# Adding the S5 state outputs in their bank by products with the identity, with u5 in halves

## The chip, the cores and the metric

The kernel runs on one core of a Trainium2 chip. The metric is the device time of one execution in microseconds (us); lower is better. A core has five engines that run side by side and meet only at semaphores: TensorE (PE, matmuls, with its weight loads shown apart as PEld), VectorE (DVE), ScalarE (ACT), GpSimd (POOL) and SyncE (SP), which here only issues DMAs. PE writes to PSUM, eight banks of 128 x 512 f32; DVE and ACT read them out.

## The reference

One step of a one-layer decoder on 256 prompt tokens and 8 x 8 sample tokens (T = 320 columns), all in f32: RMS norm, a mixer of two branches, attention over a memory of 256 tokens, and a mixture of 32 experts. The change is in the second branch of the mixer, S5, a diagonal complex state space model on 64 groups of 16 channels with 64 states each:

```python
lam_bar = jnp.exp(lam * step)
b_bar = ((lam_bar - 1.0) / lam)[..., None] * lax.complex(b_re, b_im)
bu = jnp.einsum('gnk,blgk->blgn', b_bar, ug)
bu = bu.at[:, 0].add(lam_bar * h0)
_, states = lax.associative_scan(combine, (a, bu), axis=1)     # x[l] = lam_bar * x[l-1] + bu[l]
y = jnp.real(jnp.einsum('gkn,blgn->blgk', c, states)) + d * ug
```

Here ug is u5, one slice of the input projection `rms_norm(x) @ w_in`. The first branch, SSD, takes other slices: xbc (1536 channels, a causal convolution over 4 tokens and silu), dt (softplus) and z.

## The kernel before

**S5 by chunks.** The tokens are cut into chunks of Q = 8, which gives 40 chunks (NCK): 32 of the prompt and 8 of the samples. u5T holds u5 by position in the chunk: 128 partitions x (8 positions, 8 tiles of 128 channels, 40 chunks). Three steps make the output:

- `chunk_in` (jobs hi0 to hi7, L1670): the input of each state in a chunk, by products of a table with ug. ug is u5T regrouped: SP writes u5T to DRAM (L639) and reads it back in eight pieces (L642). hi0 to hi3 need channels of the tiles 0 to 3 only, hi4 to hi7 those of the tiles 4 to 7.
- DVE: a scan over the chunks for each half of the states (`scan`, L2633 to L2644, needs hi3 or hi7) and the table of output weights (`step_out`, L2652 to L2656). `hprev` then holds the state at the start of each chunk.
- Output of a tile ft of channels, two parts. The in-chunk part, job fy (L1754), is the product of tap tables `ks` with lagged copies `ux` of u5. The part of the states is made by `chunk_out` (jobs ye and yo, L1740), copied by ACT (`chunk_states`, L1118) to yT with the chunks on the partitions, and turned by eight transposes of 40 x 128 into a second bank, job ty (L1762). ACT copies fy into u5T (L1129) and DVE adds ty to it (L2709).

The tap tables are made on PE (`taps`, jobs kk0 and kk1, L1703), masked by DVE into `tapm` (L2682, L2686), and copied within SBUF into `ks` by 16 small DMAs, 8 of them issued by SP (L663) and 8 by ACT (L1104). `ux` comes by DMA from a second copy of u5 in DRAM by tile (L651 writes, L647 reads). Three of four ux buffers lie free early; the fourth lies over tapm, so POOL clears its edge (L893) only after the copies into ks, and SP loads it then. The tiles 4 to 7 reuse the buffers: SP waits for fy of four tiles before.

**What sets the order.** Every engine has its instructions written out by hand in one order. PE's jobs are listed in `plan()`, and a job n takes bank n modulo 6, so PE waits until the job six places before has been read out. Between the S5 jobs stand the projections of the memory's keys (mk0 to mk7) and values (mv0 to mv3), transposes of the input table (bt0 to bt15), and the first projections of the SSD branch (xbc0 to xbc3), whose convolution is one step on ACT, three on DVE and a silu on ACT. After the S5 outputs come the keys' transposes (ko), the cumulative sums of dt (job cs, L1795 and L1796), which need the softplus of dt, and then long rows of split products (L1786 to L1788, L1960 to L1962) that fill PE up to the attention. The experts' weights (192 MB) are loaded by SP into buffers as they come free. SP works in order: a wait in its list holds all that stand behind it.

Of the kernel before, what the change touches and what calls it, by code (L numbers as in the profile page):

```python
# [6 lines left out]
F32 = mybir.dt.float32  # L7
# [166 lines left out]
for _name, _, _ in BLOCKS[SPLIT0:]:  # L174
# [5 lines left out]
    [f"mk{m}" for m in range(4)] + [f"bt{q}" for q in range(8)] + ["mk4", "mk5", "mk6"] + [f"hi{q}" for q in range(4)]  # L180
# [5 lines left out]
def plan():  # L186
# [8 lines left out]
    j += ["xbc0", "xbc1", "dtT", "xbc2", "dt3", "kk0", "kk1", "xbc3"]  # L195
    for n in range(3):
        j += [f"ye{n}", f"yo{n}"]
    for ft in range(KT):
        j += [f"fy{ft}", f"ty{ft}"]
        if ft == 1:  # L200
            j += ["ye3", "yo3"]
# [76 lines left out]
def layer(nc, a, o):  # L278
    ctx = ExitStack()
    with ctx:  # L280
# [299 lines left out]
        def _(sp):  # L580
# [57 lines left out]
            sp.wait_ge(s["rooted"], 2)  # L638
            sp.dma_start(scr, u5T.rearrange("p j t c -> p (j t c)")).then_inc(s["u5_out"], 16)  # L639
            sp.wait_ge(s["u5_out"], 16)  # L640
            for g in range(8):
                sp.dma_start(ug[:, g], scr.rearrange("(g k) (j f) -> g j k f", k=S5K, j=Q)[g]).then_inc(s["s5_in"], 16)  # L642
# [11 lines left out]
            sp.wait_ge(s["u5_out"], 16 + 16 * KT)  # L654
# [6 lines left out]
            for k in range(2):  # L661
# [11 lines left out]
            got(sp, "ty7")  # L673
# [128 lines left out]
        def _(pool):  # L802
# [87 lines left out]
            pool.wait_ge(s["s5_in"], 16 * (Q + 16))  # L890
# [33 lines left out]
        def _(act):  # L924
# [164 lines left out]
            for m in range(4):  # L1089
# [33 lines left out]
            conv_silu(2)  # L1123
            chunk_states(1)
            chunk_states(2)
            for ft in range(KT):
# [8 lines left out]
                if ft == 4:  # L1135
                    act.wait_ge(s["ld_small"], 16 * 8)
                    act.activation(anegb, alog[:, :], ACT.Exp).then_inc(s["sp_e"], 1)
                    act.wait_ge(s["dtx"], 1)
                    q(act.activation(dtl, dte, ACT.Exp))
                    act.activation(dtl, dtl, ACT.Ln, bias=1.0).then_inc(s["sp_e"], 1)  # L1140
# [2152 lines left out]
```

## Time and profile before

| | |
|---|---|
| median of 3 runs | 1061.39 us (1059.91 to 1068.91) |
| the profiled execution | 1062.06 us, span 1060.2 us |
| PE busy | 920.8 us, 87% |
| DVE, ACT, POOL busy | 44%, 31%, 6% |
| DMA | 304.33 MB, mean 287 GB/s |
| mean granted clock of TensorE | 0.926 |

The rows further below are lines of the profile. Times are us from the start of the span. In a timeline the columns are start, duration (of the whole run of merged instructions), engine, line, operation, tiles and shapes, and a count; a bracket gives the idle time of the engine ahead of it and what ended it. "SPq" and "ACTq" are the DMA issues of an engine. A plain f32 product shows as two records, a transpose as one. Matmuls overlap, so the distance between two starts is the pace, not the duration of one.

### The profile page before, as it was taken

Reading aid. Unit: us, or ns where it says so; the run is one execution under the profiler, and the core shown is the slowest. Engines: PE = TensorE matmul, PEld = TensorE weight load, DVE = VectorE, ACT = ScalarE, POOL = GpSimd, SP = SyncE. Lnnn points to the kernel's source line nnn. Section 1 sums busy time; section 2 is a strip of 40 time slices with the busy share of each in tenths; the row PEclk is TensorE's granted clock in tenths of the full one; section 3 lists DMA queues with packets and bytes.
Section 4 is the critical chain, followed back from the end, with each engine's and each line's share of the span. In section 5 each row is a group of like instructions: output and inputs, shape, how many; then the busy total and the mean of one; then the engine's idle time right before and its main releaser. Section 6 shows DMA issues by size and latency. Waiting matters only on the chain.

```text
span 1060.2 us, 16111 instructions
## 1 busy us (share of the span) xinstructions
PE 920.8 (87%) x6687; PEld 616.1 (58%) x6687; DVE 465.8 (44%) x793; ACT 333.7 (31%) x672; POOL 61.5 (6%) x92
## 2 busy tenths in 40 slices
PE   8998998999999999999999999677677686776584
PEld 6787476985589999989778654232222223232121
DVE  4998975757766446655665401202002020202023
ACT  5343137756475245454443511000000000000003
POOL 2701500011100000000000000000000000000000
PEclk9999998999999999999999999878788788888688
DMA  9639546545464843426799899999999999999993
GB/s 281 170 112 242 163 138 197 183 112 168 117 206 153 317 159 133 156 82 220 280 351 356 311 352 405 429 427 428 427 428 427 429 427 426 428 428 427 428 418 139
DMA packets 96212, 304.33 MB, mean 287 GB/s; under 512 B 29053, under 2 KB 44121, under 8 KB 81676
## 3 DMA queue, kind: packets, MB, share of 16 engines
q1 hardware_dynamic: 93012, 295.39, 72.9%
q0 software_dynamic: 2112, 7.28, 2.1%
q8 instruction: 54, 0.88, 0.3%
q10 hardware_dynamic: 1016, 0.62, 0.3%
q14 instruction: 18, 0.15, 0.0%
HBM read 291.02 MB, written 11.21 MB: 285 GB/s over the span
## 4 chain that ended last, share of the span: by engine, by line
PE 66%; DMA 25%; ACT 3%; DVE 2%; SPq 1%; issue 1%; ACTq 1%; DVEq 0%
DMA work<-in_w_exp_up_dram 11%; PE bank L2308 9%; DMA work<-in_w_exp_gate_dram 7%; PE bank L1564 7%; DMA work<-in_w_exp_down_dram 5%; PE bank L1960 5%; PE bank L1961 5%; PE bank L1962 5%; PE bank L1549 5%; PE bank L2354 3%; PE bank L2326 3%; PE bank L1573 3%; PE bank L1851 2%; PE bank L1971 2%; PE bank L1972 1%; PE bank L1973 1%
## 5 line engine op out<-in xcount | busy, mean ns | idle before, releaser
L2308 PE MATMUL bank<-ring,work 128*32 128x512 f32 x704 | 139.2, 698 | 70.5 <-DMA work<-in_w_exp_up_dram 24.6
L2308 PEld LDWEIGHTS bank<-ring,work 128*32 128x32 f32 x704 | 34.7, 126 | 156.6 <-issue 122.0
L1960 PE MATMUL bank<-ops,usplit 128*128 128x320 f32 x368 | 114.5, 311 | 1.1 <-DVE usplit L2822 1.1
L1961 PE MATMUL bank<-ops,usplit 128*128 128x320 f32 x368 | 113.9, 310 | 0.0
L1962 PE MATMUL bank<-ops,usplit 128*128 128x320 f32 x368 | 113.9, 309 | 0.0
L2326 PE MATMUL bank<-ring,work 128*32 128x512 f32 x416 | 65.7, 702 | 40.3 <-DMA ring<-in_w_exp_down_dram 27.7
L2822 DVE TENSOR_TENSOR usplit<-ring,usplit 128x2048 fp32r<-128x2048 f32 x31 | 71.0, 2289 | 52.9 <-ACT usplit L1235 52.9
L3149 DVE TENSOR_TENSOR work<-bank,g 128x512 f32<-128x512 f32 x7 | 4.8, 692 | 202.3 <-PE bank L2354 202.3
L2308 PE MATMUL bank<-work 128*32 128x512 f32 x304 | 87.5, 709 | 0.0
L1564 PE MATMUL bank<-work,ring 128*128 128x320 f32 (+1 forms) x304 | 76.5, 411 | 0.0
L1235 ACT ACTIVATE usplit<-ring 128x2048 fp32r<-128x2048 f32 x32 | 61.4, 1920 | 41.4 <-PE bank L1962 31.6
L1960 PEld LDWEIGHTS bank<-ops,usplit 128*128 128x128 f32 x368 | 69.2, 188 | 2.3 <-issue 2.0
L1961 PEld LDWEIGHTS bank<-ops,usplit 128*128 128x128 f32 x368 | 69.1, 188 | 0.1
L1962 PEld LDWEIGHTS bank<-ops,usplit 128*128 128x128 f32 x368 | 69.1, 188 | 0.0
L2354 PE MATMUL bank<-work 128*128 128x128 f32 (+1 forms) x384 | 68.8, 308 | 0.0
L1564 PEld LDWEIGHTS bank<-work,ring 128*128 128x128 f32 x304 | 57.3, 190 | 18.0 <-issue 1.4
L2354 PEld LDWEIGHTS bank<-work 128*128 128x128 f32 (+1 forms) x384 | 52.2, 188 | 26.6 <-issue 12.6
L2326 PEld LDWEIGHTS bank<-ring,work 128*32 128x32 f32 x416 | 17.4, 127 | 82.9 <-issue 69.0
L3171 DVE COPY work<-bank 128x512 f32<-128x512 f32 x8 | 5.5, 691 | 111.5 <-PE bank L2326 111.5
L1549 PEld LDWEIGHTS bank<-ident,work 128*128 128x128 f32 (+4 forms) x300 | 33.2, 139 | 25.5 <-issue 22.1
L1549 PE MATMUL bank<-ident,work 128*128 128x128 f32 (+4 forms) x300 | 45.7, 276 | 1.5 <-DVE work L3164 1.4
L1479 ACT ACTIVATE work<-bank 128x512 f32<-128x512 f32 x8 | 4.8, 597 | 134.1 <-PE bank L2308 134.1
(518 smaller groups left out, 1615.8 us busy)
## 6 DMA issues: line engine op xcount, KB each, us to landing
ring<-in_w_exp_down_dram SPq DMA_DIRECT2D x20, 2048.0 KB, 20.3
ring<-in_w_exp_gate_dram SPq DMA_DIRECT2D x18, 2048.0 KB, 16.1
ring<-in_w_exp_up_dram SPq DMA_DIRECT2D x16, 2048.0 KB, 20.0
ring<-in_w_in_dram SPq DMA_DIRECT2D x10, 2048.0 KB, 9.1
work<-in_w_exp_up_dram SPq DMA_DIRECT2D x8, 2048.0 KB, 28.6
work<-in_w_exp_gate_dram SPq DMA_DIRECT2D x6, 2048.0 KB, 22.2
ring<-in_w_exp_gate_dram SPq DMA_DIRECT2D x11, 1024.0 KB, 7.4
ring<-in_w_glu_dram SPq DMA_DIRECT2D x4, 2048.0 KB, 8.6
```

The source lines that it names most:

```text
L1235: act.activation(uhi[u % 2], unit_raw(u), ACT.Copy).then_inc(s["whi"], 1)
L1549: return nc.tensor.transpose(out, in_, ident[0:rows, 0:rows])
L1564: ins = nc.tensor.matmul(b[:, 0:N], wv[:, k, P * (m % 4):P * (m % 4 + 1)], src[:, k, 0:N], start=(k == 0), stop=(k == KT - 1))
L1573: ins = nc.tensor.matmul(b[0:R, :], src[:, k, P * c:P * c + R], wv[:, k, :], start=(k == 0), stop=(k == KT - 1))
L1851: ins = nc.tensor.matmul(psum[6 + (m - 3) % 2][:, 0:T], blk(f"z{m // 4}")[:, k, P * (m % 4):P * (m % 4 + 1)], hnT[:, k], start=(k == 0), s ...
L1960: nc.tensor.matmul(b[:, 0:T], wh, hi_[:, k], start=(k == 0), stop=False)
L1961: nc.tensor.matmul(b[:, 0:T], wh, lo_[:, k], start=False, stop=False)
L1962: ins = nc.tensor.matmul(b[:, 0:T], wl, hi_[:, k], start=False, stop=(k == KT - 1))
L2308: ins = nc.tensor.matmul(psum[part][ES * x:ES * (x + 1), :], xs[i % 2][:, kk, x], wt[x][:, k], start=(kk == 0), stop=(kk == KT - 1))
L2326: ins = nc.tensor.matmul(psum[2 + n_][ES * x:ES * (x + 1), :], hhT[:, j, x], wd[x][:, k, BLK * n_:BLK * (n_ + 1)], start=(j == 0), stop=(j ...
L2354: ins = nc.tensor.matmul(b[:, P * (j0 + j):P * (j0 + j + 1)], tn[0:R, c, k0 + j], sel[i % 2][0:R, c].rearrange("p x n -> p (x n)"), start= ...
L2822: TT(ulo[u % 2], unit_raw(u), uhi[u % 2].bitcast(F32), ALU.subtract).then_inc(s["wlo"], 1)
```

## The change

- The state part is added in the bank of the in-chunk part: fy is left open (`stop=False`), and the eight transposes become eight plain f32 products of yT with the identity that accumulate on it. Job ty, its bank and the adds on DVE are gone; ACT's copy of fy is the result.
- u5 goes to DRAM and back in two halves, tiles 0 to 3 and 4 to 7. SP waits for each half of the scaling; the second half's gathers also wait for the first's.
- On PE hi0 to hi3 come ahead of mk5 and mk6; xbc3 comes behind the three first `chunk_out`; `chunk_out(3)` comes behind fy3, not behind fy1.
- All 16 copies into ks are issued by SP.
- ACT and DVE are reordered: the softplus of dt goes ahead of the S5 outputs, as does conv(3).

Left out below are the changes of name in the waits on ty7 and of counts in waits on s5_in and u5_out.

```diff
 STAGE = (
-    [f"mk{m}" for m in range(4)] + [f"bt{q}" for q in range(8)] + ["mk4", "mk5", "mk6"] + [f"hi{q}" for q in range(4)]
+    [f"mk{m}" for m in range(4)] + [f"bt{q}" for q in range(8)] + ["mk4"] + [f"hi{q}" for q in range(4)] + ["mk5", "mk6"]
...
             load_block(BIDX["mk1"])
-            sp.wait_ge(s["rooted"], 2)
-            sp.dma_start(scr, u5T.rearrange("p j t c -> p (j t c)")).then_inc(s["u5_out"], 16)
-            sp.wait_ge(s["u5_out"], 16)
-            for g in range(8):
-                sp.dma_start(ug[:, g], scr.rearrange("(g k) (j f) -> g j k f", k=S5K, j=Q)[g]).then_inc(s["s5_in"], 16)
+            for half in range(2):
+                tiles, cols = slice(KT // 2 * half, KT // 2 * (half + 1)), slice(KT // 2 * NCK * half, KT // 2 * NCK * (half + 1))
+                sp.wait_ge(s["rooted"], 2 + half)
+                sp.dma_start(scr.rearrange("p (j f) -> p j f", j=Q)[:, :, cols], u5T[:, :, tiles].rearrange("p j t c -> p j (t c)")).then_inc(
+                    s["u5_out"], 16)
+                sp.wait_ge(s["u5_out"], 16 * (half + 1))
+                if half:
+                    sp.wait_ge(s["s5_in"], 16 * 8)
+                for g in range(8):
+                    sp.dma_start(ug[:, g, cols], scr.rearrange("(g k) (j f) -> g j k f", k=S5K, j=Q)[g][:, :, cols]).then_inc(s["s5_in"], 16)
...
             sp.wait_ge(s["tapm"], 1)
-            for k in range(2):
+            for k in range(4):
                 for lag in range(4):
                     sp.dma_start(ks[32 * lag:32 * lag + 32, k], tapm[32 * k:32 * k + 32, 3 - lag::4]).then_inc(s["s5_in"], 16)
...
-            for m in range(4):
+            for m in range(3):
                 conv_in(m)
...
-                if m == 2:
-                    act.wait_ge(s["tapm"], 1)
-                    for k in range(2, 4):
-                        for lag in range(4):
-                            act.dma_start(ks[32 * lag:32 * lag + 32, k], tapm[32 * k:32 * k + 32, 3 - lag::4]).then_inc(s["s5_in"], 16)
+            act.wait_ge(s["ld_small"], 16 * 8)
+            act.activation(anegb, alog[:, :], ACT.Exp).then_inc(s["sp_e"], 1)
+            act.wait_ge(s["dtx"], 1)
+            q(act.activation(dtl, dte, ACT.Exp))
+            act.activation(dtl, dtl, ACT.Ln, bias=1.0).then_inc(s["sp_e"], 1)
...
             chunk_states(0)
-            conv_silu(2)
             chunk_states(1)
             chunk_states(2)
+            conv_in(3)
+            first_tap(3)
+            conv_silu(2)
             for ft in range(KT):
...
-                if ft == 1:
+                if ft == 3:
                     conv_silu(3)
                     chunk_states(3)
-                if ft == 2:
                     pair_high(0)
...
                     for k in range(4):
                         ins = nc.tensor.matmul(b[32 * k:32 * k + 32, cols:T], ks[:, k, 1 - late, ft], ux[ft % 4][:, k, 0:T - cols],
-                                               start=(late == 0), stop=(late == 1))
-                end(ins, f"fy{ft}")
-                b = take(f"ty{ft}")
+                                               start=(late == 0), stop=False)
                 done(pe, f"ye{ft // 2}")
                 done(pe, f"yo{ft // 2}")
                 rows = slice(64 * (ft % 2), 64 * (ft % 2) + NCK)
                 for i in range(Q):
-                    ins = nc.tensor.transpose(b[:, NCK * i:NCK * (i + 1)],
-                                              yT[ft // 2][rows, Q - 1 - i].rearrange("p s h k -> p (s h k)"), ident[rows, rows])
-                end(ins, f"ty{ft}")
-
+                    ins = nc.tensor.matmul(b[:, NCK * i:NCK * (i + 1)], yT[ft // 2][rows, Q - 1 - i].rearrange("p s h k -> p (s h k)"),
+                                           ident[rows, rows], start=False, stop=(i == Q - 1))
+                end(ins, f"fy{ft}")
             for n_ in range(3):
                 chunk_out(n_)
+            proj("xbc", 3, hnT, T)
             for ft in range(KT):
                 chunk_sum(ft)
-                if ft == 1:
+                if ft == 3:
                     chunk_out(3)
...
-            u5_rooted(0)
+            u5_rooted(0).then_inc(s["rooted"], 1)
...
-            def chunk_outputs(ft):
-                done(dve, f"fy{ft}")
-                got(dve, f"ty{ft}")
-                v = u5T[:, :, ft]
-                emptied(TT(v, v, bank(f"ty{ft}")[:, 0:T].rearrange("p (j c) -> p j c", j=Q), ALU.add), f"ty{ft}")
...
             got(dve, "yo1")
             q(dve.tensor_copy(xhi, hnT))
-            for ft in range(KT):
-                chunk_outputs(ft)
...
+            conv(3)
+            got(dve, "yo3")
+            TT(xlo, hnT, xhi.bitcast(F32), ALU.subtract).then_inc(s["xlo"], 1)
+            pair_low(0)
```

## Rows read from the trace of the kernel before

**Rows 1.** The page, busy time, share of the span and instructions of each engine.

```profile
PE 920.8 (87%) x6687; PEld 616.1 (58%) x6687; DVE 465.8 (44%) x793; ACT 333.7 (31%) x672; POOL 61.5 (6%) x92
```

**Rows 2.** Windows: busy us (count) of PE, PEld, DVE, ACT, POOL; granted clock; DMA share; GB/s.

```profile
600.00:1060.00 460.00, 333.83 (x2093) 130.98 (x2092) 72.25 (x141) 45.33 (x90) 0.00 (x0) 0.84 0.96 405
```

**Rows 3.** Timeline of PE, place one and after.

```profile
71.82 10.53 PE L1564 MATMUL bank<-work,ring 128*128 128x256 f32 x48
...
85.15 5.48 PE L1670 MATMUL bank<-work,ring 128*64 128x40 f32 x128 [2.81 <-issue]
...
97.66 3.93 PE L1670 MATMUL bank<-work,ring 128*64 128x40 f32 x128
```

**Rows 4.** Timeline of the DMA queue of SP.

```profile
69.42 0.33 SPq L639 DMA_DIRECT2D u_scratch<-work  x1
...
74.59 4.97 SPq L642 DMA_DIRECT2D work<-u_scratch  x8
...
90.26 7.87 SPq L600 DMA_DIRECT2D ring<-in_w_mem_v_dram  x2
...
150.46 5.75 SPq L663 DMA_DIRECT2D work<-work  x8
...
158.96 1.78 SPq L647 DMA_DIRECT2D work<-u_by_tile  x4
```

**Rows 5.** Windows, columns as above, two stretches of low clock.

```profile
88.00:91.00 3.00, 3.00 (x62) 2.95 (x60) 0.00 (x0) 0.92 (x3) 0.00 (x0) 0.67 1.27 147
...
162.00:164.00 2.00, 2.00 (x24) 1.19 (x16) 0.00 (x0) 1.93 (x5) 0.00 (x0) 0.50 1.01 230
```

**Rows 6.** Timeline of PE, place two and after.

```profile
147.79 4.57 PE L1564 MATMUL bank<-work,ring 128*128 128x320 f32 x16
...
152.29 3.70 PE L1740 MATMUL bank<-ring,work 64*40 64x128 f32 x128
...
158.48 1.02 PE L1754 MATMUL bank<-ring,work 128*32 128x320 f32 x16
...
165.18 3.53 PE L1740 MATMUL bank<-ring,work 64*40 64x128 f32 x64 [0.97 <-issue]
...
168.64 1.02 PE L1754 MATMUL bank<-ring,work 128*32 128x320 f32 x16
...
169.59 0.69 PE L1762 MATMUL bank<-ident,ring 40*128 40x40 f32 x8
...
170.21 1.02 PE L1754 MATMUL bank<-work 128*32 128x320 f32 x16
...
177.63 1.02 PE L1754 MATMUL bank<-work 128*32 128x320 f32 x16 [1.10 <-DMA work<-u_by_tile]
...
180.99 0.29 PE L1795 MATMUL bank<-early,upto 128*128 128x16 f32 x2
...
181.14 0.37 PE L1796 MATMUL bank<-early,ones 128*128 128x16 f32 x2
...
181.36 0.38 PE L1795 MATMUL bank<-early,upto 128*128 128x16 f32 x2
```

**Rows 7.** Timeline of DVE: u5's first half, the first scan, the last tap table.

```profile
51.59 3.30 DVE L2530 TENSOR_TENSOR work<-work,ring 128x1280 f32<-128x1280 f32 x1
...
91.20 1.23 DVE L2633 TENSOR_TENSOR ring<-ring,work 128x1024 f32<-128x1024 f32 x1 [4.21 <-ACT ring L1052]
...
149.70 0.74 DVE L2686 SCALAR_TENSOR_TENSOR work<-fold,vec,work 128x32 f32<-128x32 f32 x4
```

**Rows 8.** Timeline of ACT, its DMA issues.

```profile
150.47 5.41 ACTq L1104 DMA_DIRECT2D work<-work  x8
```

**Rows 9.** Timeline of POOL, the instruction that waits for the tap tables' copies.

```profile
157.74 1.19 POOL L893 MEMSET work<- 32x160 f32 x3 [26.62 <-DMA work<-work]
```

**Rows 10.** Weight loads of PE by shape: busy us, mean ns of one, then idle before.

```profile
L1762 PEld LDWEIGHTS bank<-ident,ring 40*128 40x128 f32 x48 | 3.8, 151 | 2.1 <-ACT ring L1118 1.0 <-issue 1.0
...
L1879 PEld LDWEIGHTS bank<-work,ident 32*128 32x128 f32 x32 | 2.4, 182 | 1.8 <-issue 1.8
```

More of the change, by code:

```diff
@@ L194, in plan @@
     j += STAGE
-    j += ["xbc0", "xbc1", "dtT", "xbc2", "dt3", "kk0", "kk1", "xbc3"]
+    j += ["xbc0", "xbc1", "dtT", "xbc2", "dt3", "kk0", "kk1"]
     for n in range(3):
         j += [f"ye{n}", f"yo{n}"]
+    j.append("xbc3")
     for ft in range(KT):
-        j += [f"fy{ft}", f"ty{ft}"]
-        if ft == 1:
+        j.append(f"fy{ft}")
+        if ft == 3:
             j += ["ye3", "yo3"]
@@ L653, in _ @@
             load_block(BIDX["mv1"])
-            sp.wait_ge(s["u5_out"], 16 + 16 * KT)
+            sp.wait_ge(s["u5_out"], 16 * 2 + 16 * KT)
             sp.wait_ge(s["uxz"], 1)
@@ L671, in _ @@
             load_block(BIDX["z1"])
-            got(sp, "ty7")
+            got(sp, "fy7")
             done(sp, "s5o1")
@@ L888, in _ @@
             pool.dma_start(o["mv"][0, 0].rearrange("(c p) a d -> p c (a d)", p=P), vm).then_inc(s["out_s5"], 16)
-            pool.wait_ge(s["s5_in"], 16 * (Q + 16))
+            pool.wait_ge(s["s5_in"], 16 * (2 * 8 + 16))
             pool.wait_ge(s["sls"], 1)
@@ L1129, in _ @@
                 emptied(act.activation(u5T[:, :, ft], bank(job)[:, 0:T].rearrange("p (j c) -> p j c", j=Q), ACT.Copy), job)
-                if ft == 1:
+                if ft == 3:
                     conv_silu(3)
                     chunk_states(3)
-                if ft == 2:
                     pair_high(0)
[L1135 to L1140, printed above, removed]
             pair_high(1)
@@ L1290, in _ @@
                 if m == 4:
-                    done(act, "ty7")
+                    done(act, "fy7")
                     act.activation(u5_hi, u5T, ACT.Copy).then_inc(s["u5_hi"], 1)
@@ L1660, in chunk_in @@
                 b = take(f"hi{i}")
-                if i == 0:
-                    pe.wait_ge(s["s5_in"], 16 * Q)
+                if i % 4 == 0:
+                    pe.wait_ge(s["s5_in"], 16 * 8 * (i // 4 + 1))
                 if i % 4 == 0:
@@ L1709, in _ @@
             pe.wait_ge(s["rot"], 1)
-            for m in range(4):
+            for m in range(3):
                 proj("xbc", m, hnT, T)
@@ L1748, in chunk_sum @@
                 b = take(f"fy{ft}")
-                pe.wait_ge(s["s5_in"], 16 * (Q + 16))
+                pe.wait_ge(s["s5_in"], 16 * (2 * 8 + 16))
                 pe.wait_ge(s[f"ux{ft % 4}"], 64 * (ft // 4 + 1))
@@ L2689, in lag_taps @@
                     ins.then_inc(s["tapm"], 1)
-            for m in range(4):
+            for m in range(3):
                 conv(m)
@@ L2713, in pair_low @@
                 TT(ulo[u % 2], pair_raw(u), uhi[u % 2].bitcast(F32), ALU.subtract).then_inc(s["elo"], 1)
+            dve.wait_ge(s["dtx"], 1)
+            q(TS(dtm, dtx, 0.0, None, ALU.max))
+            dve.wait_ge(s["sp_e"], 2)
+            q(TT(dt_, dtm, dtl, ALU.add))
+            STT(out=dtA, in0=dt_, scalar=-1.0, in1=anegb.unsqueeze(1).to_broadcast([P, NC, HEADS]),
+                op0=ALU.mult, op1=ALU.mult).then_inc(s["dt_ready"], 1)
             got(dve, "yo1")
             q(dve.tensor_copy(xhi, hnT))
-            for ft in range(KT):
-                chunk_outputs(ft)
-                if ft == 1:
-                    got(dve, "yo3")
-                    TT(xlo, hnT, xhi.bitcast(F32), ALU.subtract).then_inc(s["xlo"], 1)
-                if ft == 3:
-                    pair_low(0)
-                if ft == 5:
-                    dve.wait_ge(s["dtx"], 1)
-                    q(TS(dtm, dtx, 0.0, None, ALU.max))
-                    dve.wait_ge(s["sp_e"], 2)
-                    q(TT(dt_, dtm, dtl, ALU.add))
-                    STT(out=dtA, in0=dt_, scalar=-1.0, in1=anegb.unsqueeze(1).to_broadcast([P, NC, HEADS]),
-                        op0=ALU.mult, op1=ALU.mult).then_inc(s["dt_ready"], 1)
+            conv(3)
+            got(dve, "yo3")
+            TT(xlo, hnT, xhi.bitcast(F32), ALU.subtract).then_inc(s["xlo"], 1)
+            pair_low(0)
             got(dve, "cs")
```

2 lines of the change are left out of this document (1 added, 1 removed).

## The prediction

> **What bounds the kernel now.** I read the page first: TensorE (PE) is busy for 87% of the span [rows 1]. The windows by stage then show two regimes. From 600 us on the DMA engines are busy 96% of the time at 405 GB/s, and PE only 333.8 us of 460 [rows 2]: there the kernel is a chain of expert loads, and SP issues each when PE has freed its buffer. That tail starts when PE lets it. Ahead of it PE is the bound, and everything that the change edits lies before 185 us. So I looked in the timeline of PE for the places where it pauses or is slow, and asked the timelines of SP, DVE and ACT what ends each.
>
> Place one. PE stands still for 2.81 us before the first chunk products (L1670, hi0 to hi3) [rows 3]. The profile puts it down to "issue"; the kernel waits there on s5_in, the gather of u5 through DRAM, and SP issued those gathers only from 74.59 to 79.56 [rows 4]. The clock is low right after the pause, 0.67 granted at 88 to 91, so mostly at 1.2 in place of 2.4 GHz [rows 5]. hi0 to hi3 last 5.48 us, the same work of hi4 to hi7 3.93 [rows 3].
>
> Place two, the S5 outputs (jobs fy and ty), from 158.48 to the cumulative sums at 180.99: 22.5 us [rows 6]. At full clock a pair takes 170.21 - 168.64 = 1.57, of which ty, eight transposes, is 170.21 - 169.59 = 0.62 and fy 0.95. Eight pairs are 12.6; chunk_out(3) is half of the 3.70 that two take, 1.85; the keys' transposes take 180.99 - (177.63 + 1.57) = 1.8 [rows 6]. That makes 16.2. The other 6.3 are pauses (1.10 before fy7, 0.97 before chunk_out(3)) and low clock: 0.50 granted at 162 to 164, and chunk_out(3) takes 3.53 [rows 5, 6].
>
> **u5 in halves, hi0 to hi3 ahead of mk5 and mk6.** DVE has scaled the first half of u5 by 51.59 + 3.30 = 54.9, the second by 69.4 [rows 7]. Before, one write to DRAM (issued 69.42, gathers 5.2 later) and eight gathers (4.97) followed the second [rows 4]. Now the first half is written at 54.9, gathered from about 60 to 65, and there by about 71, even if write and landing take all of the 5.2 and 5.6 (79.56 to 85.15) that they took for the whole. PE reaches hi0 after mk4, a third of the 10.53 us of mk4 to mk6: 71.82 + 3.5 = 75.3 [rows 3]. The pause goes and the low clock with it: 2.81 + (5.48 - 3.93) = 4.4 us. The second half is there by 85, and hi4 wants it at 97.66 - 4.4 = 93.3: hidden, with 8 us to spare.
>
> SP gets one write, eight gathers and two waits more. What queues behind them are the eight writes by tile and the load of mv0, issued at 90.26 [rows 4]. SP had nothing to issue from 55 to 69.4, and the second half's part is no longer than the old whole, so mv0 is not later. But PE wants it behind hi4 to hi7, at 97.66 + 3.93 - 4.4 = 97.2 [rows 3]. I charge nothing; if its landing binds, up to 1.5 us of the gain is lost.
>
> **What the gain moves.** DVE idles 4.21 us for hi3 before its first scan at 91.20 [rows 7]. The scan starts at 87.0 now, and DVE's work from there to the tap tables, 149.70 + 0.74 = 150.44 [rows 7], moves by 4.2, to 146.2. PE agrees: the taps end at 147.79 where xbc3 starts [rows 6], so 143.4 now, and the tables come 2.7 behind them as before. Less would follow if only one of the two moved; both do.
>
> **The tap tables' copies (ks).** Before, SP issued 8 in 5.75 us and ACT 8 beside it in 5.41 [rows 4, 8]. SP's last issue ended at 156.2, and POOL, which waits for all, went on at 157.74: 1.5 to land [rows 9]. Now SP issues all 16. At 5.75 / 8 = 0.72 this takes 11.5: 146.2 + 11.5 + 1.5 = 159.2 for fy0, where it was 158.48. The front's gain is spent here, and 0.7 more. For one queue issuing alone this shape has no row. The nearest row at the low end is four other 32-partition copies that SP issued alone in 1.78, 0.445 each [rows 4]; the high end is 0.72. I take 0.72, the row of the same copy. Queued behind them on SP are the loads of ux[3] and of the tiles 4 to 7 by lag; the first is ready at about 165, and fy3 starts at 159.2 + 3 x 2.7 = 167.3, so they stay hidden.
>
> The Trainium skill, "DMA: Bandwidth & Descriptors", section "Rules for kernel authors", says that spreading DMAs over SP, ACT and GpSimd gives no bandwidth, since all run on the same 16 engines, and saves only the sequencer's issue time. It speaks against the change: the issue time is what binds here. By that rule the eight moved copies cost their full 5.8 us. The trace shows two queues at once and not one with 16, so it neither confirms nor denies it.
>
> PE meanwhile does the taps to 143.4, three chunk_out (3 x 1.85) and xbc3, now behind them (4.5, from 147.79 to 152.29), to 153.5 [rows 6]. It then pauses 5.7 us for the copies. The 2.81 us pause of place one was followed by low clock that cost 1.55; I charge that once, 1.6.
>
> **The products with the identity.** A transpose of 40 x 128 took 0.62 / 8 = 0.077 us and leaves one record; a plain f32 product leaves two, each with its weight load. 128 records take the place of 64. Their price: the cumulative sums (128x128 weights, 16 columns) start every 181.36 - 181.14 = 0.22 for 2 records, 0.11 each [rows 6]. A plain load of 128 columns lasts 182 ns even with 32 rows of weights, a transpose's 151 at 40 rows [rows 10]. So the loads set the pace, and the plain form, 0.11, is nearer than 0.077: 16 x 0.11 = 1.76 a tile in place of 0.62. A tile is 0.95 + 1.76 = 2.71, eight are 21.7, 9.1 more than before. Low end 0.077 (17.4 for eight); high end 0.182, were no load overlapped (30.9), which the sums' row speaks against.
>
> The Trainium skill, "TensorE: Matmul & The Clock Gate", section "LDWEIGHTS (loading the stationary operand)", has a load take its columns over 1.2 GHz whatever its rows, 107 ns here; by that the tile costs 1.71 and the sum is 0.4 us lower. The trace agrees for plain products, and not for the transposes at 77 ns. It too speaks against the change: 40 rows load no faster than 128.
>
> **What is removed.** Eight adds on DVE and eight banks. DVE was not the bound there. PE's pauses for ACT go, since ACT is free of 5.41 us of issues and has its copies done in PE's long pause; that is in the sum, which has no other pause. The 1.10 before fy7 goes too: its load needs fy3's end plus some 6.5 us (170.21 + 0.95 to 177.63), and chunk_out(3) with three tiles is now 1.85 + 8.1 = 10 us [rows 6]. The softplus of dt and conv(3) are moved into the pause of PE on ACT and DVE, at no cost. Were that cover gone, they would cost ACT about what fits between 142 and 157 now, a few us, ahead of the copies of ye and yo.
>
> **The sum.** 159.2 + 21.7 + 1.85 + 1.8 + 1.6 = 186.2 for the cumulative sums, in place of 180.99: 5.2 later. From there I pass the delay on whole, since PE paces all that follows. The profiled execution took 1062.06 us (span 1060.2), 0.7 above the median of the runs, 1061.39. On the median: 1061.39 + 5.2 = 1066.6.
>
> **The rivals.**
> 1. One queue issues as fast as two together, the faster side. At 0.445: 146.2 + 7.1 + 1.5 = 154.8, PE pauses 1.3 and keeps its clock, 154.8 + 25.4 = 180.2: 0.8 earlier, 1060.6. It decides at 0.49 an issue. For it: that row, and that the two queues' eights took the same time, as if they shared something. Against: it is another copy. Chance 0.17.
> 2. Products at the transposes' pace, 0.077: 159.2 + 17.4 + 3.65 + 1.6 = 181.9, 0.9 later, 1062.3. For: the same 40 x 128 block. Against: 182 ns a load. Chance 0.12.
> 3. The tail hides it: if the loads before 600 have slack, 1061.4. Against: the tail is full from its start [rows 2], so what starts late ends late. Chance 0.08.
> 4. The clock stays low, or the loads don't overlap. Mild: the low clock of place two again, 1.68 on chunk_out(3) (3.53 - 1.85) beside the 1.6: 1068.3. Hard: all 25.4 us of the stage at the ratio 5.48 / 3.93 = 1.4 is 10.2 in place of 1.6, 1075.2; loads at 0.182 give 9.2, 1075.8. For: a long pause ahead of a stage of small products. Against: place one recovered in about 5 us. Chance 0.13 (mild 0.03, hard 0.10).
>
> Of rival 4 the same page of the Trainium skill says, in "Part 4: PE-mode transpose", that transposes do not count as busy for the clock; by that the new code would hold its clock better than the old. No row here separates it, and no number above uses it.
>
> The forecast has 0.47; 0.03 is for more than 1% faster by none of these.
>
> **How the numbers follow.** 1% is 10.6 us, about what a measurement of this kernel can tell from no change. The forecast, rivals 1 to 3 and the mild form lie within it, 0.87; slower 0.10, the hard form at 13.8 us and more; faster 0.03. The range reaches from rival 1 with 2 us for its landing terms, 1058.5, to 1074.5, just short of the hard form; the forecast's own is 1063 to 1070.
>
> **What will show it.** No pause before L1670 at about 75; first scan at 87; 16 copies on SP from 146 to 157.7 (to 153.4 in rival 1); a pause of 5.7 before fy0 at 159 and low clock behind it; 16 records in 1.76 us a tile (1.24 in rival 2); cumulative sums at 186. I am wrong if the copies or the products are off by a third, or if all of that holds and the end does not move (rival 3).

## The result, and the profile after

The changed kernel takes 1090.01 us (median of 4 runs, 1083.47 to 1090.42), the kernel before 1063.52 (4 runs, 1059.91 to 1068.91). The ratio is 1.023, 95% interval 1.0200 to 1.0261: slower by 2.3%. Forecast were 1066.6, a range of 1058.5 to 1074.5, 0.87 for no measurable change and 0.10 for slower. The profiled execution of after took 1090.42 us (span 1088.6).

The page of after, busy time by engine (compare [rows 1]):

```profile
PE 949.1 (87%) x6751; PEld 638.6 (59%) x6751; DVE 461.3 (42%) x785; ACT 334.2 (31%) x672; POOL 60.4 (6%) x92
```

PE has 64 records more, as the forecast says (128 in place of 64), and is busy 28.3 us longer. The share stays 87%.

The timeline of PE in after, the front and then the S5 outputs (answers to [rows 3, 6]):

```profile
74.75 3.93 PE L1671 MATMUL bank<-work,ring 128*64 128x40 f32 x128
...
148.85 4.57 PE L1565 MATMUL bank<-work,ring 128*128 128x320 f32 x16
160.01 1.83 PE L1755 MATMUL bank<-ring,work 128*32 128x320 f32 x16 [6.59 <-issue]
161.76 3.63 PE L1761 MATMUL bank<-ident,ring 40*128 40x40 f32 x16
...
181.29 3.65 PE L1741 MATMUL bank<-ring,work 64*40 64x128 f32 x64
184.87 1.83 PE L1755 MATMUL bank<-ring,work 128*32 128x320 f32 x16
186.62 2.06 PE L1761 MATMUL bank<-ident,work 40*128 40x40 f32 x16
188.61 1.02 PE L1755 MATMUL bank<-ring,work 128*32 128x320 f32 x16
189.56 3.04 PE L1761 MATMUL bank<-ident,work 40*128 40x40 f32 x16
...
203.17 3.67 PE L1550 MATMUL bank<-ident,work 128*128 128x128 f32 x16
206.64 0.44 PE L1794 MATMUL bank<-early,upto 128*128 128x16 f32 x2
```

The front is as forecast: hi0 to hi3 at 74.75 with no pause, in 3.93 us. So is the way to fy0: 160.01, after a pause of 6.59. The DMA queue of SP in after shows what the pause waits for (compare [rows 4]), 16 copies at 0.74 us each:

```profile
146.64 11.84 SPq L669 DMA_DIRECT2D work<-work  x16
```

Then the stage goes wrong. It lasts 206.64 - 160.01 = 46.6 us; it took 22.5 before and was forecast at 27.0. The windows of after (busy us and count of PE, PEld, DVE, ACT, POOL; granted clock; DMA share; GB/s) say why:

```profile
160.00:166.00 6.00, 5.99 (x40) 4.48 (x44) 0.00 (x0) 0.44 (x1) 1.05 (x3) 0.50 0.33 89
...
178.00:184.00 6.00, 6.00 (x68) 5.85 (x72) 0.00 (x0) 0.89 (x3) 0.00 (x0) 0.50 0.46 118
...
188.00:190.00 2.00, 2.00 (x27) 1.42 (x27) 0.63 (x1) 1.78 (x2) 0.00 (x0) 1.00 1.05 396
190.00:192.00 2.00, 2.00 (x13) 2.00 (x12) 1.66 (x1) 0.00 (x0) 0.00 (x0) 0.56 0.26 99
192.00:206.00 14.00, 14.00 (x81) 11.44 (x82) 0.00 (x0) 3.60 (x6) 0.00 (x0) 0.50 0.01 2
```

PE is busy all the time and waits for nothing, yet its granted clock is 0.50, the 1.2 GHz level. It comes up only briefly, at 186.8 behind chunk_out(3), and falls again at 190.2 with no pause ahead of it. A tile costs 1.75 for fy and 3.57 for the products, 5.32 us, where 2.71 was forecast. The clock is back at 207.3, right behind the keys' transposes (L1550), as this window shows:

```profile
207.00:208.00 1.00, 1.00 (x10) 0.97 (x9) 0.00 (x0) 0.48 (x1) 0.22 (x1) 0.85 0.00 0
```

Behind the stage the delay is passed on: the first split product starts at 208.18 (before 182.22), 26.0 later; a later product of the SSD branch (L1889) and the next split products (L1959) stand 26.0 later too; the first expert product (L2307) 27.1; the end of the span 28.4.

### The profile page after: what moved, and what is told of

Same layout as the page of the kernel before. It is cut to its first block, busy times and chain, and to the rows that moved or that the text cites. A ratio compares the mean times of both kernels' runs of the same rounds, so it can differ in the third digit from the quotient of the medians.

```text
span 1088.6 us, 16234 instructions
## 1 busy us (share of the span) xinstructions
PE 949.1 (87%) x6751; PEld 638.6 (59%) x6751; DVE 461.3 (42%) x785; ACT 334.2 (31%) x672; POOL 60.4 (6%) x92
## 4 chain that ended last, share of the span: by engine, by line
PE 56%; DMA 24%; DVE 11%; SPq 5%; issue 2%; ACT 1%; DVEq 0%; ACTq 0%
DMA ring<-in_w_exp_down_dram 12%; PE bank L2307 7%; DMA ring<-in_w_exp_gate_dram 7%; DMA ring<-in_w_exp_up_dram 5%; PE bank L1959 5%; PE bank L1960 5%; PE bank L1961 5%; PE bank L1550 4%; PE bank L2325 4%; PE bank L2353 3%; PE bank L1761 2%; PE bank L1850 2%; SPq L605 2%; PE bank L1970 2%; PE bank L1971 1%
## 5 line engine op out<-in xcount | busy, mean ns | idle before, releaser
L2307 PE MATMUL bank<-ring,work 128*32 128x512 f32 x704 | 140.3, 702 | 68.8 <-DMA work<-in_w_exp_up_dram 22.6
L2307 PEld LDWEIGHTS bank<-ring,work 128*32 128x32 f32 x704 | 34.8, 127 | 154.2 <-issue 121.8
L1959 PE MATMUL bank<-ops,usplit 128*128 128x320 f32 x368 | 114.5, 311 | 1.1 <-DVE usplit L2811 1.1
L2307 PE MATMUL bank<-work 128*32 128x512 f32 x304 | 87.3, 708 | 0.0
L1959 PEld LDWEIGHTS bank<-ops,usplit 128*128 128x128 f32 x368 | 69.2, 188 | 2.3 <-issue 2.0
L1550 PEld LDWEIGHTS bank<-ident,work 128*128 128x128 f32 (+4 forms) x300 | 34.7, 143 | 25.1 <-issue 21.6
L1550 PE MATMUL bank<-ident,work 128*128 128x128 f32 (+4 forms) x300 | 47.3, 284 | 1.5 <-DVE work L3153 1.4
## 6 DMA issues: line engine op xcount, KB each, us to landing
work<-in_w_exp_up_dram SPq DMA_DIRECT2D x8, 2048.0 KB, 28.4
```

The source lines that it names most:

```text
L1550: return nc.tensor.transpose(out, in_, ident[0:rows, 0:rows])
L1959: nc.tensor.matmul(b[:, 0:T], wh, hi_[:, k], start=(k == 0), stop=False)
L2307: ins = nc.tensor.matmul(psum[part][ES * x:ES * (x + 1), :], xs[i % 2][:, kk, x], wt[x][:, k], start=(kk == 0), stop=(kk == KT - 1))
```

## The experiments

Twelve kernels ran; kernel n below is the one of experiment n. Each ratio is to runs of the kernel before that were taken beside it and whose median lay between 1063.2 and 1064.4 us. "Stage" is from fy0 to the first split product, its start and end in the profiled run (in the last two the sums of dt stand ahead of the stage); "clock" is the mean granted clock from fy0 to the cumulative sums, or to the first split product for the last two.

| kernel | stage | clock | median us | ratio to before (95%) |
|---|---|---|---|---|
| before | 158.48 to 182.22 | 0.85 | | 1 |
| after | 160.01 to 208.18 | 0.54 | 1090.01 | 1.0230 (1.0200 to 1.0261) |
| 1 after, with transposes | 159.99 to 185.40 | 0.70 | 1064.61 | 1.0009 (0.9989 to 1.0029) |
| 2 before, with plain products | 161.78 to 199.99 | 0.73 | 1081.02 | 1.0152 (1.0101 to 1.0204) |
| 3 after, pause filled | 159.79 to 201.91 | 0.63 | 1085.37 | 1.0181 (1.0137 to 1.0226) |
| 4 after, products 80 wide | 160.09 to 199.08 | 0.68 | 1082.53 | 1.0182 (1.0131 to 1.0232) |
| 5 both 3 and 4 | 159.11 to 196.62 | 0.72 | 1078.21 | 1.0139 (1.0119 to 1.0159) |
| 6 3, and dense products between | 159.22 to 195.52 | 1.00 | 1074.90 | 1.0093 (1.0059 to 1.0126) |
| 7 dense products between alone | 160.62 to 204.79 | 0.80 | 1083.02 | 1.0165 (1.0137 to 1.0192) |
| 8 before, with the new front | 155.37 to 179.28 | 0.85 | 1061.49 | 0.9980 (0.9962 to 0.9998) |
| 9 1, copies on two queues | 164.07 to 186.12 | 0.89 | 1064.96 | 1.0011 (0.9993 to 1.0029) |
| 10 1, chunk_out(3) early | 159.44 to 186.44 | 0.71 | 1066.24 | 1.0018 (0.9998 to 1.0038) |
| 11 combination | 156.44 to 181.11 | 0.71 | 1059.14 | 0.9938 (0.9910 to 0.9965) |
| 12 11, pause filled | 155.51 to 177.76 | 0.79 | 1057.92 | 0.9936 (0.9916 to 0.9955) |

**1. Which part costs the time?** The kernel after, with the eight transposes, their bank and DVE's adds put back. The single queue for the copies and the long pause stay.

```diff
-                    ins = nc.tensor.matmul(b[:, NCK * i:NCK * (i + 1)], yT[...], ident[rows, rows], start=False, stop=(i == Q - 1))
+                    ins = nc.tensor.transpose(b[:, NCK * i:NCK * (i + 1)], yT[...], ident[rows, rows])
```

> The changed kernel with its products with the identity put back to the eight transposes per tile, their second bank and the adds on DVE; halves, job order and the 16 copies on SP stay, so PE's pause of 6.6 us ahead of fy0 stays too. Theory A (the pause sends the clock to 1.2 GHz, and the plain products of 40 columns keep it there): with transposes the clock is back at 2.4 GHz after one or two stretches, as in the kernel before, so the stage takes 16.2 us and some 3 to 4 of low clock, the cumulative sums start at about 180 and the time is that of before within 3 us. Rival B (after such a pause any small work keeps the clock low, whatever its form): a pair is 1.83 + 1.07 = 2.9 us throughout, the stage about 31 us, the sums at 191, the time 10 us above before.

Measured: 1064.61, ratio 1.0009. The plain products are the whole loss that can be measured: 1090.0 - 1064.6 = 25.4 us (23.5 by the two ratios). The rest of the change is neutral, though its pause is the same. The time is as theory A had it; the sums stand at 184.18, 4 us later than it said. PE's timeline of this kernel:

```profile
159.99 1.83 PE L1755 MATMUL bank<-ring,work 128*32 128x320 f32 x16 [6.46 <-issue]
161.74 1.07 PE L1763 MATMUL bank<-ident,ring 40*128 40x40 f32 x8
...
171.03 3.55 PE L1741 MATMUL bank<-ring,work 64*40 64x128 f32 x64
174.50 1.02 PE L1755 MATMUL bank<-ring,work 128*32 128x320 f32 x16
175.45 0.68 PE L1763 MATMUL bank<-ident,work 40*128 40x40 f32 x8
```

The clock is low here too, for all of the first four tiles (2.76 us each), so the transposes do not bring it back. It returns with the end of chunk_out(3), at 174.3, and then it stays: tiles of 1.56. In after it came back just behind the same job and fell again.

**2. The products alone.** The kernel before with only this: the transposes become plain products into the same second bank. DVE's adds stay.

```diff
-                    ins = nc.tensor.transpose(b[:, NCK * i:NCK * (i + 1)], yT[...], ident[rows, rows])
+                    ins = nc.tensor.matmul(b[:, NCK * i:NCK * (i + 1)], yT[...], ident[rows, rows], start=True, stop=True)
```

> The kernel before with only its 64 transposes of yT turned into plain products with the identity, into the same second bank, with the adds on DVE left. The pauses there are short (1.1 us at most). Theory A with the pause as the needed start: about 9 us more PE work at full clock and, as the kernel before already has a stretch of low clock in this stage from 161, which the plain products would prolong, 9 to 25 us above before. Rival C (products alone): a tile 5.3 us for most of the stage, 20 to 25 us above before. Rival B (the form does not matter, only the pause): 9 us above before and the low clock ends at about 168 as before.

Measured: 1081.02, ratio 1.0152, within the wide range of theory A and below that of rival C. No pause in the stage is longer than 0.6 us, and the clock is 2.4 GHz from 172 to 182. PE's timeline of this kernel:

```profile
180.41 1.02 PE L1754 MATMUL bank<-ring,work 128*32 128x320 f32 x16
181.36 3.23 PE L1762 MATMUL bank<-ident,work 40*128 40x40 f32 x16
184.52 1.83 PE L1754 MATMUL bank<-ring,work 128*32 128x320 f32 x16
186.27 3.63 PE L1762 MATMUL bank<-ident,ring 40*128 40x40 f32 x16
```

At 181.8, 0.4 us into the first products shown, the pace halves, with no idle time since 168.5, and it stays so to the end of the keys' transposes. So with these products the clock falls without any pause ahead of it, and it does so although they don't add up on fy's bank here. A tile at 2.4 GHz, from one fy to the next, takes 2.85 here as well.

**3. The pause.** The kernel after, with 28 products of 128 x 128 by 128 columns between xbc3 and fy0; they add work whose result nobody reads.

```diff
             proj("xbc", 3, hnT, T)
+            warm(psum[7][:, 0:P], 28)
```

> The changed kernel with 28 dummy products (128x128 of ones, 128 columns, result unused) between xbc3 and fy0, about 6 us, so that PE is busy through the wait for the tap tables' copies. Nothing else moves. Theory A (the pause starts the low clock): the clock is at 2.4 GHz when fy0 starts at about 160, a tile takes 0.95 + 1.76 to 2.0 us, the stage about 26 us, sums at 186, time 5 to 7 us above before. Rival C (the plain products bring the clock down by themselves, pause or not): a few tiles at full clock, then 5.3 us each again; sums at 200 or later, time 18 us or more above before.

Measured: 1085.37, 4.6 us less than after. PE's timeline of this kernel:

```profile
159.79 1.02 PE L1755 MATMUL bank<-ring,work 128*32 128x320 f32 x16 [0.37 <-issue]
160.73 1.97 PE L1761 MATMUL bank<-ident,ring 40*128 40x40 f32 x16
162.64 1.02 PE L1755 MATMUL bank<-ring,work 128*32 128x320 f32 x16
...
169.78 1.83 PE L1755 MATMUL bank<-work 128*32 128x320 f32 x16
171.54 3.63 PE L1761 MATMUL bank<-ident,ring 40*128 40x40 f32 x16
```

The stage starts at full clock, with tiles of 2.85 us, of which the products take 162.64 - 160.73 = 1.91, 0.119 a record. 7 us later, at 166.7, the clock falls, and fy and its products take 1.76 and 3.56. The sums stand at 200.54, as rival C had it. The pause explains only how the low clock begins.

**4 and 5. More columns per product.** Each product takes 80 columns of the identity in place of 40; the other 40 are zeros that are added to a neighbour. Alone, and with the pause filled.

```diff
+                    lo, hi = (i, min(i + 2, Q)) if ft % 2 == 0 else (max(i - 1, 0), i + 1)
+                    eye = ident[rows, rows.start - NCK * (i - lo):rows.start + NCK * (hi - i)]
```

> The changed kernel with each product of yT taken against 80 columns of the identity's rows in place of 40, the 40 more adding zeros to the neighbouring chunk position; results are the same. The pace is set by the loads (0.22 us for a product at 2.4 GHz, 0.45 at 1.2), so 80 columns cost nothing by themselves: 2 x 80 columns are 0.13 us at 1.2 GHz. Theory A in its finer form (the clock stays low because PE streams too few columns in this stage): the clock comes back within two or three tiles, and the time falls by 10 us or more below the changed kernel. Rival D (the loads or the form of the instruction hold it low, not the columns): no change, 1090.

> Both remedies at once in the changed kernel: 28 dummy products through the pause ahead of fy0, and 80 columns of the identity per product. If the pause and the few columns are the two causes of the low clock (what filling alone and widening alone suggest: the first held 2.4 GHz for 7 us only, the second kept it once it was back at 184), the clock stays at 2.4 GHz over the whole stage: a tile 2.85 us as in the widened kernel after 184, the stage 8 x 2.85 + 3.65 = 26.5 from 160, sums at 186.5, time 5 to 7 us above before (1069). If something else holds it low, a stretch at 1.2 GHz remains and the sums come at 195 or later, 1078 or more.

Measured: 1082.53 and 1078.21. At full clock the wide products take no longer (1.90 to 1.94 a tile), and there is less low clock. But the effect is no clean one: alone, the first four tiles are still at 1.2 GHz and the last four, behind chunk_out(3), at 2.4; with the pause filled the clock still falls at 165 and again at 189. Neither came where its theory had it: kernel 4 gained 7.5 us in place of 10 or more, and kernel 5 has its sums at 195.11, on the side of "something else". It helps and does not cure, and I draw no rule from it.

**6 and 7. Dense work between the products.** Four dense products as in experiment 3 behind each tile, results unused, once with the pause filled and once without.

```diff
             for ft in range(KT):
                 chunk_sum(ft)
+                warm(psum[7][:, 0:P], 4)
```

> The kernel after, with the pause of TensorE filled (28 products of 128 x 128 by 128 columns, results unused) and with 4 more such products behind each tile, results unused. The filled kernel without them took 1085.4 us: its tiles began at full clock (2.85 us a tile) and the clock fell by itself at 166.9; its cumulative sums stood at 200.5. Theory (products of 40 rows by 40 columns, bound by their weight loads, let the clock fall however busy TensorE is, and dense products in between keep it up): a tile costs 2.85 + 0.9 = 3.75 at 2.4 GHz throughout, chunk_out(3) 1.85 and the keys' transposes 1.8, so the cumulative sums come at 159.8 + 30 + 3.65 = 193.5, 7 us earlier than in the filled kernel although there is 7.2 us more work, and the time is 1078 to 1079. Rival (the clock falls some 7 to 10 us into the stage whatever stands between the products, as a limit on power would have it): tiles of 5.3 + 1.3 us for most of the stage, cumulative sums at 207 or later, time 1091 or more.

> The kernel after with its pause before fy0 as it is, and only the 4 dense products (128 x 128 by 128 columns, results unused) behind each tile. Tells the pause from the make-up of the stage. With pause filled and the same mix the clock was 2.4 GHz all through, a tile cost 3.94 and the cumulative sums stood at 194.3. Theory A (the make-up of the stage decides; the pause only gives the fall at its start): fy0 at 160.0 at 1.2 GHz, about one and a half tiles of 5.3 + 2.2 = 7.5 us there, then full clock to the end: cumulative sums at 198 to 201, time 1078 to 1082, below the 1090.0 of the kernel after in spite of about 8.7 us of added work. Theory B (once low, the clock stays low in the stage as it did in the kernel after, so the pause is the cause): eight tiles of 7.5 us, cumulative sums at 220 or later, 1100 or more.

Measured for 6: 1074.90, 10.5 us less than experiment 3, with 8 x 1.09 = 8.7 us more work in it. PE's timeline and one window of this kernel:

```profile
160.17 1.98 PE L1761 MATMUL bank<-ident,ring 40*128 40x40 f32 x16
162.08 1.16 PE L1582 MATMUL bank<-ones 128*128 128x128 f32 x8
163.16 1.02 PE L1755 MATMUL bank<-ring,work 128*32 128x320 f32 x16
...
194.29 0.29 PE L1796 MATMUL bank<-early,upto 128*128 128x16 f32 x2
...
170.00:180.00 10.00, 10.00 (x147) 8.41 (x147) 2.83 (x1) 4.26 (x9) 0.00 (x0) 1.00 0.68 198
```

The clock is 2.4 GHz from end to end, the tile 3.94 us, and the sums come at 194.29, as the first theory had it (193.5); the time is 3 us below its range. A limit that strikes after some time whatever is run is ruled out.

Measured for 7: 1083.02, 7 us less than after in spite of the added work. The windows of this kernel:

```profile
172.00:175.00 3.00, 3.00 (x15) 2.92 (x14) 0.00 (x0) 0.44 (x1) 0.00 (x0) 0.50 0.18 50
175.00:178.00 3.00, 3.00 (x24) 1.61 (x24) 0.00 (x0) 0.00 (x0) 0.00 (x0) 0.56 0.49 127
178.00:181.00 3.00, 3.00 (x32) 2.55 (x35) 0.00 (x0) 0.44 (x1) 0.00 (x0) 1.00 0.19 48
```

The clock comes back and stays, ahead of chunk_out(3) this time. So with the same pause the make-up of the stage decides whether the clock comes back and holds; the pause adds its own low stretch, 8.1 us of time (1083.02 against 1074.90). But the return took 17 us and two and a half tiles, not 10 and one and a half: the sums are at 203.56 in place of 198 to 201, and the time is 1 us above the range. How fast the clock returns was my weak point here as well.

**8. The front alone.** The kernel before with u5 in halves and hi0 to hi3 behind mk4, nothing else.

```diff
-    ... + ["mk4", "mk5", "mk6"] + [f"hi{q}" for q in range(4)]
+    ... + ["mk4"] + [f"hi{q}" for q in range(4)] + ["mk5", "mk6"]
...
+            for half in range(2):
```

> The kernel before with only the front of the change: u5 in halves, hi0 to hi3 behind mk4. Transposes, adds, both queues for the copies, order of the S5 outputs as before. Forecast of the front: no pause ahead of hi0, first scan about 3.7 us earlier, tap tables at 146.6 for 150.4, so the time is 3.5 to 4.4 us below before (0.996). Rival: the gain is lost behind, in a new pause ahead of mv0 or in another phase of the low clock: within 1 us of before.

Measured: 0.9980 (0.9962 to 0.9998), some 2 us, about half of what was expected. The cumulative sums stand at 178.05, 2.9 us earlier than before, of the 4.4 that the front gives; the rest goes into waits of PE ahead of the third and the fourth chunk_out (1.46 and 1.80 us, where they were 0.59 and 0.97).

**9 and 10. What else might have eaten the gain.** Both start from kernel 1. In 9 half of the copies goes back to ACT, ahead of its copies of ye and yo. In 10 chunk_out(3), with ACT's copies of it, is back behind fy1.

```diff
+            act.wait_ge(s["tapm"], 1)
+            for k in range(2, 4):
+                for lag in range(4):
+                    act.dma_start(ks[32 * lag:32 * lag + 32, k], tapm[32 * k:32 * k + 32, 3 - lag::4]).then_inc(s["s5_in"], 16)
...
-                if ft == 3:
+                if ft == 1:
```

> The changed kernel with the transposes, the second bank and the adds back, and the copies into ks split again over SP and ACT, 8 each. The copies are there at about 146.6 + 5.75 + 1.5 = 153.9, PE's pause is 0.5 us in place of 6.5. Theory: without the pause the clock holds at 2.4 GHz, the stage takes about 17 to 18 us from 154, sums at 172 to 173 for 181 before, time 7 to 8 us below before. Rival (transposes of 40 columns let the clock fall as the plain products do): a stretch of 1.2 GHz in the stage, sums at 177 to 180, time 1 to 4 us below.

> The changed kernel with transposes back and one copy queue, and chunk_out(3) behind fy1, where the kernel before has it, not behind fy3. In all traces so far the clock came back during or right behind chunk_out(3) (168.5 in before, 174.5 with transposes back). If that job is what lifts it, it is at 2.4 GHz by about 169 here, two tiles earlier, and the time is 2 to 3 us below the kernel with transposes back (1062). If the return only takes its time after the pause, the clock is back at about 174 again and the time is the same, 1064 to 1065.

Kernel 9 missed its expectation: 1064.96, no gain. ACT issues the copies where PE needs it for ye and yo, and PE's pause moves ahead of xbc3, as its timeline in this kernel shows:

```profile
156.79 7.34 PE L1569 MATMUL bank<-work,ring 128*128 128x320 f32 x16 [8.49 <-ACT ring L1128]
164.07 1.02 PE L1759 MATMUL bank<-ring,work 128*32 128x320 f32 x16
```

The pause sends the clock low here too, but the products of xbc3 run behind it, and it is back at 162.4, ahead of fy0. The stage with transposes then holds 2.4 GHz for 17 us, to 179.5, where PE has just waited 0.70 us for a load of ux and 0.75 for DVE.

In 10 the clock returns 5 us earlier, at 169.3, right behind chunk_out(3), as its timeline of PE and one window show:

```profile
164.96 3.65 PE L1741 MATMUL bank<-ring,work 64*40 64x128 f32 x64
168.54 1.38 PE L1755 MATMUL bank<-ring,work 128*32 128x320 f32 x16
...
169.00:170.00 1.00, 1.00 (x19) 0.48 (x11) 0.00 (x0) 0.96 (x3) 0.00 (x0) 0.84 0.05 15
```

The job was moved and the return moved with it, so it follows the job and not the time since the pause. The gain in time that was expected with it, 2 to 3 us, did not come. Then fy7 waits 1.08 us for its load of ux, the wait that the late chunk_out(3) had covered, ty7 waits 0.89 for DVE, and the clock falls once more, at 179.6. Ratio 1.0018: no gain.

**11 and 12. A version that beats both.** The new front; transposes and DVE's adds as before; the copies issued by SP (11) and POOL (5), which has nothing else to do there; xbc3 and the sums of dt ahead of fy0; chunk_out(3) behind fy1. In 12 the split is 9 and 7, with four dense products, results unused, behind the sums of dt.

```diff
+            for i in range(11, 16):
+                k, lag = divmod(i, 4)
+                pool.dma_start(ks[32 * lag:32 * lag + 32, k], tapm[32 * k:32 * k + 32, 3 - lag::4]).then_inc(s["out_s5"], 16)
```

> The parts that the study found good, with the eight transposes a tile, their second bank and the adds on VectorE as in the kernel before: u5 in halves and hi0 to hi3 early, the copies into ks split between SyncE (11) and GpSimd (5), xbc3 and the cumulative sums of dt ahead of fy0, chunk_out(3) behind fy1. Theory (what the front gained, 4.2 us, was spent on one queue for 16 copies and then on low clock): the copies have landed at 146.2 + 11 x 0.72 + 1.5 = 155.6, fy0 starts there in place of 160.0, TensorE pauses about 1.5 us in place of 6.5, and the tiles take 1.57 at 2.4 GHz or up to 2.76 for a few of them; the split products begin 3 to 5 us earlier than before, the time is 1057 to 1059, faster by 0.2 to 0.4%. Rival (GpSimd's queue is slow to issue, or the clock is low for the whole stage as with the plain products): the split products begin no earlier than before, 1061 to 1064.

> The kernel of the last run of this kind (transposes kept; u5 in halves; copies into ks by SyncE and GpSimd; xbc3 and the sums ahead of fy0), with the copies split 9 and 7 in place of 11 and 5, and 4 dense products, results unused, in the rest of the pause before fy0. There 11 copies took 8.39 us on SyncE and 5 took 3.78 on GpSimd beside it, 0.76 each on both; fy0 began at 156.44 after a pause of 2.03, at 1.2 GHz until 166, and chunk_out(3) took 3.65. Theory: the copies are there 1.5 us earlier, 154.9, the pause is gone, and the stage begins at 2.4 GHz: tiles of 1.57, chunk_out(3) 1.85, the split products begin some 5 us earlier than in that run unless the waits before fy7 grow by the same; time 1055 to 1058, ratio 0.990 to 0.994. Rival (what starts the stage earlier is taken back by the wait of fy7 for its load of ux, 1.13 us there, which follows fy3 by some 6.5 us): ratio 0.993 to 0.996.

Measured: 0.9938 (0.9910 to 0.9965) and 0.9936 (0.9916 to 0.9955), both faster than before by 0.6%; they can't be told apart, and 0.9936 lies in the range of the theory and in that of the rival. Kernel 12's DMA queues of SP and POOL, then its PE:

```profile
146.16 6.98 SPq L668 DMA_DIRECT2D work<-work  x9
...
146.44 4.84 POOL L898 DMA_DIRECT2D work<-work  x7 [19.69 <-DVE work L2693]
...
155.51 1.02 PE L1760 MATMUL bank<-ring,work 128*32 128x320 f32 x16
156.46 0.69 PE L1768 MATMUL bank<-ident,ring 40*128 40x40 f32 x8
...
164.29 1.02 PE L1760 MATMUL bank<-ring,work 128*32 128x320 f32 x16 [0.57 <-DMA ring<-u_by_tile]
```

Two queues side by side keep 0.78 and 0.69 us an issue, as SP alone had 0.74, so the pace is each queue's own. The pause is gone, and the first tiles are at full clock. Part of it is given back: fy4, fy5 and fy6 now wait for their loads of ux (0.57, 0.70 and 0.66), and the clock falls at 168.5, in the last of these waits. The first split product comes at 177.76, 4.5 us earlier than before; the span is 4.1 shorter. In 11 the split products begin only 1.1 us earlier than before, where 3 to 5 were expected, and the profiled span is 1059.2 (before 1060.2), while the median of the runs gains more; one profiled run doesn't resolve this.

## Why the prediction was wrong

**The front: right.** hi0 to hi3 at 74.75 (75.3 forecast), first scan at 87.52 (87.0), tap tables done at 146.6 (146.2), nothing lost on mv0.

**The copies: right.** 0.74 an issue (0.72), fy0 at 160.0 (159.2), pause 6.6 (5.7). Rival 1 falls: an issue takes no less on one queue alone than on two at once. The Trainium skill, "DMA: Bandwidth & Descriptors", section "Rules for kernel authors", has more queues save issue time and nothing else. Kernels 11 and 12 agree as to the issue time, with 0.69 to 0.78 an issue on two queues at once against 0.74 on one.

**The products at full clock: nearly right.** 1.90 a tile (1.76), a tile 2.85 (2.71), 1.1 us more for eight. Rival 2 falls: 0.119 a record, not 0.077.

**The clock: the step that failed.** The prediction says: "The 2.81 us pause of place one was followed by low clock that cost 1.55; I charge that once, 1.6." At full clock the stage would be 8 x 2.85 + 1.9 + 1.8 = 26.5 us; it took 46.6. The term is 20.1, not 1.6, and this is nearly all of the miss at the sums (206.6 against 186.2: 18.5 of 20.4). Two things were wrong in it.

First the cause. I took low clock for the echo of a pause, with a price per pause. Experiment 3 removes the pause and keeps most of the loss; experiment 2 loses the clock 13 us after the last idle time; 6 and 7 hold it or bring it back by changing only what stands between the products. Shown is: a stage that is mostly small products with the identity (40 rows, 40 columns) runs down to 1.2 GHz by itself while PE is busy without a gap, and its own tiles don't bring it back up. The same stage with transposes fell only in or just behind waits of PE, though short waits are enough (0.57 to 0.70 us in kernel 12). In the profiled runs the sums of after stand 206.64 - 184.18 = 22.5 us behind those of kernel 1: 10.3 are the products' own work (8 x 1.29), 13.7 are clock (20.1 in after, 6.4 in kernel 1), less 1.5 of waits that only kernel 1 has.

Second the size. Rival 4's hard form is what happened, but I priced it at the ratio 5.48 / 3.93 = 1.4. That row spans both levels (0.67 granted), so it can't give the price of the low one. The rows that could were there: chunk_out(3), 3.53 at a clock of 0.50 against 1.85, is 1.91 [rows 5, 6]; in after the tile is 5.32 / 2.85 = 1.87. With 1.87 the hard form gives 159.2 + 25.4 x 1.87 = 206.7 for the sums, which is what they were, and 1087.1 for the time. That it hits to 0.1 us is luck: fy0 was 0.8 later and the work at full clock 1.1 more than in the sum, which makes 2.9 with the ratio, and 3.4 us of the stage at full clock took 3.0 of it back. The argument against the hard form, that place one recovered in about 5 us, came from other products: those of hi0 to hi3 stand 0.031 us apart (3.93 / 128) and have 128 rows, those with the identity 0.119 and 40 [rows 3].

The Trainium skill, "TensorE: Matmul & The Clock Gate", section "Part 4: PE-mode transpose", says that full clock doesn't engage for transposes, as they don't count as busy in the same way. Kernel 1 agrees for those of 40 x 128: four tiles with them did not lift the clock. But a stage with them held 2.4 GHz for 17 us (kernel 9), and in after and in kernels 2, 3 and 5 the clock came back at 207.3, 198.9, 200.8 and 195.7, right behind the keys' transposes of 128 x 128 (L1550). In kernels 9 and 10, where these ran at 1.2 GHz too, it came back only 5.8 and 5.5 us behind them, so the runs don't tell what lifted it there. What I drew from the page, that the new code would hold its clock better than the old, is false: plain products of this size lift it no better. They are also twice as many records, at 0.119 in place of 0.077 us each, and so take up 1.90 of a tile's 2.85 us in place of 0.61 of 1.56; that this share is the reason is not shown.

**The tail: right.** The delay is passed on whole (26.0 at the first split product, 28.4 at the end), so rival 3 falls. The last 2.4 us arise behind L1959 (1.1 by 637) and were not taken apart.

**What remains of the forecast.** Kernel 6 holds the clock; less its 8.7 us of added products its sums are at 185.6, 4.6 later than before, and its time at 1066.2, 2.3 above before in its comparison (1063.95). Forecast were 5.2, of them 1.6 of clock, so 3.6. Apart from the clock the change costs about what the sum says; the interval of the ratio, some 3.6 us to each side, doesn't tell more.

What the runs don't settle is which property of the work holds the clock: experiments 4 and 5 (columns) helped only in part, and rows were not varied.

## What to carry to other kernels

Before small f32 products replace something else on TensorE, read the granted clock of the stage, and work it out at both levels: 100% busy with no idle time is no sign of full clock. Take the price of the low level from a row that lies wholly in it (0.50 granted), never from one that spans a change. And when a gain at the front is spent on one queue's issues, give them to an engine that is idle there, not to one that the next jobs wait for.

## What the runs showed of the hardware

- A stage whose tiles are two thirds plain f32 products of 40 rows by 40 columns and one third fy let the granted clock fall from 1.00 to 0.50 with PE busy throughout (after at 190.2, kernel 2 at 181.8, kernel 3 at 166.7); their pace went from 0.119 to 0.223 us a record, weight loads and all.
- Once at 0.50, it did not come back during the tiles alone (after: 21 us to chunk_out(3), all at 0.50). It came back at the end of the 64 records of chunk_out(3) or within 2 us behind them (before, after and kernels 1 to 5, 8, 10 and 11; in 10, where the job was moved forward, 5 us earlier than in 1), with dense products between the tiles (7, after 17 us), and right behind the keys' transposes (after, 2, 3 and 5, but not in 9 and 10).
- Small copies within SBUF cost 0.74 us of issue each on SP alone (after), 0.76 to 0.78 on SP and 0.69 to 0.76 on POOL side by side (11, 12); the four loads of ux from DRAM cost 0.44 each on the same queue of SP.
